# Recurrent heads of a hybrid decoder step: intra-chunk products grouped by tile width, and one weight split moved ahead of the state's scaling

## The chip, the cores and the metric

The kernel runs on one core of a Trainium2 chip. The metric is device time in microseconds (us) of one launch; lower is better. The kernel before takes 1378.13 us, the median of three runs between 1377.38 and 1378.83 us.

## What is computed

The reference is one step of a decoder layer with two parallel branches over 1024 prompt tokens and 8 x 4 sample tokens: a gated linear recurrence (HGRN2, 8 heads with keys and values of 128) and a sliding-window attention. Both branches read one large input projection of the normalised tokens. The change touches the recurrence alone:

```python
def hgrn2_chunk(S, q, k, v, logf):
    b = jnp.cumsum(logf, axis=1)
    diff = b[:, :, None] - b[:, None, :]
    decay = jnp.where(causal, jnp.exp(jnp.where(causal, diff, 0.0)), 0.0)
    att = jnp.einsum('bthk,bshk,btshk->bhts', q, k, decay)
    o = jnp.einsum('bhts,bshv->bthv', att, v) + jnp.einsum('bthk,bhkv->bthv', q * jnp.exp(b), S)
    b_last = b[:, -1]
    k_dec = k * jnp.exp(b_last[:, None] - b)
    S_new = jnp.exp(b_last)[..., None] * S + jnp.einsum('bshk,bshv->bhkv', k_dec, v)
    return S_new, o

h = jnp.einsum('btd,dc->btc', xn, w_in)     # the input projection, 1024 x 8448
```

## The kernel before, in words

Every engine has its own program, written by hand, and the engines meet only through counting semaphores. An order table (class `Steps`, lines 56 to 78) names the steps of each engine, so that `pe.at(now, "os")` is the count that TensorE's semaphore reaches when its step "os" is done. Nothing is scheduled by a tool: each engine works in the order of its code.

**Blocks and slots.** The projections are made in blocks of 128 output columns over all 1056 tokens. A block has three slots of 352 tokens, one PSUM bank each (`pj`), and a slot is 24 matmuls of 128 x 128 by 352 (line 970): 8 slices of the contraction, three passes each, since a 32-bit product is put together from a rounded high part and a rest (`w_h`, `w_l`, `xn_h`, `xn_l`). ScalarE rounds a block's weights into `w_h` (`split_hi`, line 628) and GpSimd subtracts to get `w_l` (`split_lo`, line 556); the first slot of block n waits for both (lines 965 and 966). The buffers are double: `w_h`, `w_l` of block n lie where those of block n-2 lay.

**A recurrent head.** The heads 0 to 7 run one after the other; 1 to 6 are a hardware loop. In each head TensorE (function `head`, lines 1022 to 1111) mixes the small products of the recurrence with the slots of four blocks of projections for the next head: block B(0) (values), B(1) (the forget gate), B(2) and B(3) (query and output gate). The slots fill the time in which VectorE and ScalarE work for the recurrence. The order around the change on TensorE is: slot 1 of B(1); the intra-chunk products (lines 1059 to 1070); slot 2 of B(1); the sample product `ps` and the state updates `u0`, `u1` (line 1079); slots 0 and 1 of B(2); the outputs `o0`, `o1` and the sample outputs `os` (lines 1089 to 1098); slot 2 of B(2); the sample state updates `us0`, `us1` (line 1102); slot 0 of B(3), the first work that needs the weights of B(3); the means of the squares (lines 1108 and 1109, after VectorE's `so1`); slots 1 and 2 of B(3).

**The intra-chunk products.** A chunk is 128 tokens here, and there are 8 of them in two PSUM banks (`ps_a`, `ps_b`). The causal 128 x 128 block of a chunk is built of seven products, each with its own reference point for the decay, so that all exponents stay small: one of 64 x 64 (line 1062, `d64`), two of 32 x 32 next to the diagonal (line 1064, `d32`), four of 32 x 32 on the diagonal (line 1068, `dk`, `dq`). All contract over 128 rows. The output's partitions say which columns of TensorE's array work: the 64 x 64 product uses columns 0 to 63, the two `d32` products use the strips 0 to 31 and 64 to 95, and the four diagonal ones use one strip of 32 columns each. They are plain 32-bit matmuls, and the trace has two weight loads and two matmuls for each product: 16 passes of 64 columns and 96 of 32 columns in a head.

**GpSimd in a head.** The order (function `head`, lines 563 to 583) is: splits of B(0) and B(1); the sample values; `v_exp`; split of B(2); then a wait for TensorE's `os`, the scaling of the sample state (line 579, step "s0e"), and the split of B(3). VectorE adds `us0`, `us1` to the scaled state (line 1515, steps `so0`, `so1`), and between the gates and that it makes the rest of the squares, `sq_l` (line 1509). In the last head ScalarE waits for "s0e" before it rounds the heads' outputs into `hl_h` (lines 751 to 754).

Of the kernel before, what the change touches and what calls it, by code (L numbers as in the profile page):

```python
# [35 lines left out]
P = 128  # L36
# [6 lines left out]
NC = SEQ // P  # L43
# [48 lines left out]
def hybrid_step(nc, x_prompt, x_sample, state_hgrn, cache_k, cache_v, norm_in, w_in, lb_logits, a_gnorm,  # L92
# [84 lines left out]
    with ctx:  # L177
        def sb(name, shape, dt=F32, where=ctx):
            return where.enter_context(nc.sbuf_tensor(name, shape, dt))
# [6 lines left out]
        ps_a, ps_b, ps_c, ps_d, ps_e = [ctx.enter_context(nc.psum_tensor(f"ps_{n}", [P, 512], F32)) for n in "abcde"]  # L186
# [38 lines left out]
        d64 = sb("d64", [P, NC, 2, 64], where=area)  # L225
# [324 lines left out]
        @block.gpsimd  # L550
        def _(g):
            def split_lo(B):

                n, p, _ = B
                g.wait_ge(w_hi_ready, n + 1)
                g.tensor_tensor(w_l[p][:], w_raw[p][:], w_h[p][:].bitcast(F32), ALU.subtract).then_inc(w_lo_ready, 1)  # L556

            pro = Blocks(0, 1, 0)
            g.memset(eps[:], EPS).then_inc(pool_done, pool.tick(("pro", 0), "eps"))
            for n in range(3):  # L560
                split_lo(pro(n))

            def head(i):
                B, now = head_blocks(i), now_of(i)
                split_lo(B(0))
                split_lo(B(1))
                if is_first(i):
                    g.wait_ge(masks_loaded, 48)
                g.wait_ge(act_done, act.at(now, "v3_hi2"))

                g.tensor_tensor(v3[NS:2 * NS, :], v_tok[0:NS, NC, :], v3[0:NS, :].bitcast(F32), ALU.subtract).then_inc(pool_done, pool.tick(now, "v3_lo"))
                g.wait_ge(pool_done, pool.at(now, "v3_lo"))
                g.tensor_tensor(v_exp[:], v3[:].bitcast(F32).rearrange("p (o v) -> p o v", o=1).to_broadcast([3 * NS, NB, P]),
                                batch_m[:].rearrange("p (b o) -> p b o", o=1).to_broadcast([3 * NS, NB, P]),
                                ALU.mult).then_inc(pool_done, pool.tick(now, "vexp"))
                split_lo(B(2))

                g.wait_ge(pe_done, pe.at(now, "os"))
                g.tensor_tensor(s0[:], s0[:], E[:, NC:NC + NB].rearrange("p (b o) -> p b o", o=1).to_broadcast([P, NB, P]),  # L579
                                ALU.mult).then_inc(pool_done, pool.tick(now, "s0e"))  # L580
                split_lo(B(3))
                if is_last(i):
                    split_lo(B(4))

            head(0)
            with nc.gpsimd.Fori(1, HEADS - 1) as i:
                head(i)
            head(HEADS - 1)
            with nc.gpsimd.Fori(1, HEADS) as j:
                B = Blocks(GA, 2, j)  # L590
                split_lo(B(1))
                split_lo(B(2))
            for n in range(4):
                split_lo(Blocks(QZ, 2, 0)(n))
            with nc.gpsimd.Fori(0, HEADS - 1) as m:
                B = Blocks(QZ, 2, m)
                split_lo(B(4))
                split_lo(B(5))
            with nc.gpsimd.Fori(0, 4) as j:
                B = Blocks(GB, 2, j)  # L600
                split_lo(B(2))
                split_lo(B(3))

            def wo_split_lo(n):
                c = WO_ORDER[n]
                g.wait_ge(wo_hi_ready, n + 1)
                g.tensor_tensor(wo_at(c, 1), wo_raw[:], wo_at(c, 0).bitcast(F32), ALU.subtract).then_inc(wo_lo_ready, 1)

            wo_split_lo(0)
            for j in range(3):  # L610
                split_lo(Blocks(PB, 2, j)(2))
                split_lo(Blocks(PB, 2, j)(3))
                wo_split_lo(2 * j + 1)
                wo_split_lo(2 * j + 2)
            wo_split_lo(7)
# [342 lines left out]
        def _(t):  # L958
# [63 lines left out]
            def head(i):  # L1022
                B, now = head_blocks(i), now_of(i)
# [32 lines left out]
                gate_slot(1, "v", (act_done, act), 1)  # L1056

                t.wait_ge(dve_done, dve.at(now, "dkm"))
                for n, bank in enumerate((ps_a, ps_b)):
                    for j in range(4):  # L1060
                        c, o = 4 * n + j, j * P
                        nc.tensor.matmul(bank[0:64, o + 64:o + 128], d64[:, c, 0, :], d64[:, c, 1, :], start=True, stop=True)
                        for m in range(2):
                            nc.tensor.matmul(bank[64 * m:64 * m + 32, o + 64 * m + 32:o + 64 * m + 64],
                                             d32[:, 2 * c + m, 0, :], d32[:, 2 * c + m, 1, :], start=True, stop=True)
                        for m in range(4):
                            e = c * P + 32 * m
                            mm = nc.tensor.matmul(bank[32 * m:32 * m + 32, o + 32 * m:o + 32 * m + 32],
                                                  dk[:, e:e + 32], dq[:, e:e + 32], start=True, stop=True)
                    mm.then_inc(pe_done, pe.tick(now, f"p{n}"))  # L1070
# [5 lines left out]
                for n, bank in enumerate((ps_c, ps_d)):  # L1076
                    for j in range(4):
                        c = 4 * n + j
# [7 lines left out]
                for n, bank in enumerate((ps_e, ps_c)):  # L1086
                    for j in range(4):
                        c = 4 * n + j
# [12 lines left out]
                for n, bank in enumerate((ps_a, ps_b)):  # L1101
                    nc.tensor.matmul(bank[:, :], k3[:, :], v_exp[:, 4 * n:4 * n + 4, :].rearrange("p b v -> p (b v)"),
                                     start=True, stop=True).then_inc(pe_done, pe.tick(now, f"us{n}"))
# [7 lines left out]
                gate_slot(3, "q", (dve_done, dve), 2)  # L1111

            head(0)
            with nc.tensor.Fori(1, HEADS - 1) as i:
                head(i)
            head(HEADS - 1)


            t.wait_ge(act_done, act.at(("last", 0), "sg2"))
            slots(Blocks(GA, 2, 0)(1), hl_h, hl_l, split="last")  # L1120
            with nc.tensor.Fori(1, HEADS) as j:
                B = Blocks(GA, 2, j)
# [15 lines left out]
            for n, bank in enumerate((ps_a, ps_b)):  # L1138
                for j in range(4):
                    c = 4 * n + j  # L1140
# [95 lines left out]
            for u in range(4):  # L1236
                h, grp = u // 2, u % 2
                rows_h = slice(h * HD, (h + 1) * HD)
                bank, o = (ps_c, ps_d)[h], grp * 2 * P
# [18 lines left out]
            for u in range(4):  # L1258
# [3 lines left out]
                for j in range(4):  # L1262
                    o = grp * P + 32 * j
                    mm = nc.tensor.matmul(ps_e[rows_h, o:o + 32], cv[:, 4 * grp + j, rows_h], PT_s[:, u, 32 * j:32 * j + 32],
                                          start=False, stop=True, skip_group_check=True)
# [3 lines left out]
            with nc.tensor.Fori(1, 3) as j:  # L1269
                B = Blocks(GB, 2, j)  # L1270
# [18 lines left out]
            with nc.tensor.Fori(1, 3) as j:  # L1289
                B = Blocks(PB, 2, j)  # L1290
# [444 lines left out]
```

## Time and profile before

| | |
|---|---|
| median of three runs | 1378.13 us |
| span of the profiled execution, first to last instruction | 1374.8 us |
| what lies around the span (median less span) | 3.3 us |
| TensorE busy in the span | 1324.7 us, 96% |
| GpSimd busy | 259.8 us, 19% |
| mean granted TensorE clock | 0.991 of full speed |
| the eight recurrent heads | about 60 us to 565 us of the span |

Times in the rows are us from the span's start unless marked ns. PE is a TensorE matmul, PEld its weight load, DVE VectorE, ACT ScalarE, POOL GpSimd. The records of matmuls overlap, since the array is a pipeline, and their ends are modelled: what a matmul costs is read from the distance between starts. A matmul of 352 columns is recorded with 0.32 us, but one starts every 0.16 us. "x6" in a timeline means that six like instructions are merged into one row, from the first one's start to the last one's end.

### The profile page before, as it was taken

How to read it: one execution, taken by the hardware profiler on the slowest of the kernel's cores; microseconds unless marked ns; L12 is line 12 of the kernel's file. 1: busy time of each engine (PE TensorE's matmuls, PEld its weight loads, DVE VectorE, ACT ScalarE, POOL GpSimd, SP SyncE). 2: the span in 40 equal slices, each digit the busy share in tenths (PEclk: the TensorE clock that was granted, in tenths of full speed). 3: DMA queues.
4: the chain of work that ended last, by engine and by line, in shares of the span. 5: the costliest groups of instructions: out<-in, count | busy, mean ns of one | idle time of the engine just before them, and what ended most of it. 6: DMA issues, size and time to landing. Idle time of an engine off the chain costs nothing.

```text
span 1374.8 us, 23499 instructions
## 1 busy us (share of the span) xinstructions
PE 1324.7 (96%) x9150; PEld 1252.4 (91%) x9150; DVE 602.9 (44%) x1239; ACT 519.1 (38%) x1022; POOL 259.8 (19%) x119
## 2 busy tenths in 40 slices
PE   5799999999999999999999999999999999999998
PEld 4799999999999999899999988988988899999885
DVE  6636566574746465500000444555554400445222
ACT  6343635445353535511111434455444422313111
POOL 0222222222322222222222111011011022242000
PEclk9899999999999999999999999999999999999999
DMA  5212121202021221111112310111110312141231
GB/s 190 64 31 64 32 64 32 76 17 76 17 76 47 62 63 34 49 44 46 46 46 51 81 31 15 31 31 24 22 31 1 87 33 61 46 113 41 92 129 47
DMA packets 136750, 73.61 MB, mean 54 GB/s; under 512 B 37185, under 2 KB 133138, under 8 KB 136690
## 3 DMA queue, kind: packets, MB, share of 16 engines
q1 hardware_dynamic: 136706, 72.99, 19.0%
q8 instruction: 31, 0.51, 0.2%
q14 instruction: 13, 0.11, 0.0%
HBM read 63.77 MB, written 10.22 MB: 54 GB/s over the span
## 4 chain that ended last, share of the span: by engine, by line
PE 67%; issue 22%; POOL 5%; ACT 3%; DVE 3%; DMA 0%; SPq 0%; DVEq 0%; POOLq 0%; ACTq 0%
PE pj L970 46%; POOL w_l L556 4%; PE pj L986 3%; PE pj L1311 2%; PE ps_d L1201 1%; PE ps_e L1201 1%; PE ps_a L1311 1%; PE ps_e L1311 1%; PE ps_b L1189 1%; PE ps_c L1311 1%; PE ps_d L1311 1%; PE ps_b L1311 1%; PE ps_a L1189 1%; PE ps_a L1166 1%; PE ps_c L1189 1%
## 5 line engine op out<-in xcount | busy, mean ns | idle before, releaser
L970 PE MATMUL pj<-xn_h,w_h 128*128 128x352 f32 x1704 | 562.6, 330 | 10.9 <-DVE q L1384 5.3
L970 PE MATMUL pj<-xn_h,w_l 128*128 128x352 f32 x1704 | 552.0, 324 | 0.0
L970 PE MATMUL pj<-xn_l,w_h 128*128 128x352 f32 x1704 | 551.7, 324 | 0.0
L556 POOL TENSOR_TENSOR w_l<-w_raw,w_h 128x1024 fp32r<-128x1024 f32 x82 | 202.2, 2466 | 731.0 <-ACT w_h L628 731.0
L970 PEld LDWEIGHTS pj<-xn_h,w_h 128*128 128x128 f32 x1704 | 324.3, 190 | 15.7 <-DVE q L1384 5.6
L970 PEld LDWEIGHTS pj<-xn_l,w_h 128*128 128x128 f32 x1704 | 324.8, 191 | 0.3
L970 PEld LDWEIGHTS pj<-xn_h,w_l 128*128 128x128 f32 x1704 | 323.7, 190 | 0.0
L628 ACT ACTIVATE w_h<-w_raw 128x1024 fp32r<-128x1024 f32 x82 | 86.4, 1054 | 114.7 <-PE pj L970 99.8
L1546 DVE TENSOR_TENSOR mg<-sg,pj 128x352 f32 (+1 forms) x24 | 12.4, 522 | 151.7 <-PE pj L970 150.2
L837 ACT ACTIVATE scores<-scores,stat 128x256 f32<-128x256 f32 (+1 forms) x128 | 61.4, 481 | 0.0
L970 PE MATMUL pj<-hl_h,w_l 128*128 128x352 f32 x168 | 54.3, 323 | 0.0
L970 PE MATMUL pj<-hl_l,w_h 128*128 128x352 f32 x168 | 54.3, 323 | 0.0
L970 PE MATMUL pj<-hl_h,w_h 128*128 128x352 f32 x168 | 54.0, 322 | 0.0
L1384 DVE TENSOR_TENSOR zs<-zs,pj 128x352 f32<-128x352 f32 x24 | 12.5, 522 | 83.5 <-ACT zs L659 83.5
L1384 DVE TENSOR_TENSOR zb<-zb,pj 128x352 f32<-128x352 f32 x24 | 12.5, 521 | 83.5 <-ACT zb L659 83.5
L579 POOL TENSOR_TENSOR s<-s,E 128x1024 f32<-128x1024 f32 x8 | 15.2, 1897 | 173.0 <-PE ps_d L1097 173.0
L659 ACT ACTIVATE zs<-pj 128x352 f32<-128x352 f32 x24 | 11.1, 464 | 95.3 <-PE pj L970 95.3
L659 ACT ACTIVATE zb<-pj 128x352 f32<-128x352 f32 x24 | 11.1, 464 | 90.0 <-PE pj L970 90.0
L951 ACT ACTIVATE y_sq<-y_o 128x1024 f32<-128x1024 f32 (+1 forms) x9 | 9.5, 1060 | 79.7 <-DVE y_o L1674 79.7
L1389 DVE TENSOR_TENSOR xn_l<-hb,xn_h 128x1056 fp32r<-128x1056 f32 x8 | 10.3, 1304 | 63.3 <-ACT xn_h L667 63.2
L659 ACT ACTIVATE k<-pj 128x352 f32<-128x352 f32 x24 | 11.0, 464 | 70.1 <-PE pj L970 70.1
L659 ACT ACTIVATE sg<-pj 128x352 f32<-128x352 f32 x24 | 10.9, 464 | 66.6 <-PE pj L970 66.6
(363 smaller groups left out, 2095.6 us busy)
## 6 DMA issues: line engine op xcount, KB each, us to landing
w_raw<-in_w_in_dram SPq DMA_DIRECT2D x132, 256.0 KB, 3.4
x_t<-in_x_prompt_dram SPq DMA_DIRECT2D x8, 512.0 KB, 8.5
s<-in_state_hgrn_dram SPq DMA_DIRECT2D x8, 512.0 KB, 4.2
out_dram<-s SPq DMA_DIRECT2D x8, 512.0 KB, 3.2
w_raw<-in_w_pa_dram SPq DMA_DIRECT2D x16, 256.0 KB, 2.9
w_raw<-in_w_pb_dram SPq DMA_DIRECT2D x16, 256.0 KB, 4.4
wo_raw<-in_w_out_dram SPq DMA_DIRECT2D x8, 512.0 KB, 4.0
x_o<-in_x_prompt_dram SPq DMA_DIRECT2D x8, 512.0 KB, 4.1
```

Of the source, the lines that this page charges most:

```text
L556: g.tensor_tensor(w_l[p][:], w_raw[p][:], w_h[p][:].bitcast(F32), ALU.subtract).then_inc(w_lo_ready, 1)
L579: g.tensor_tensor(s0[:], s0[:], E[:, NC:NC + NB].rearrange("p (b o) -> p b o", o=1).to_broadcast([P, NB, P]), ALU.mult).then_inc(pool_done ...
L628: a.activation(w_h[p][:], w_raw[p][:], ACT.Copy).then_inc(w_hi_ready, 1)
L659: a.activation(out[:, span(g)], pj[g][:, 0:W], ACT.Sigmoid).then_inc(act_done, act.tick(where, f"{name}{g}"))
L837: a.activation(scores[:, u, keys], scores[:, u, keys], ACT.Exp, bias=stat[:, 1, u:u + 1], accum_out=stat[:, 3, u:u + 1]).then_inc(act_done ...
L970: mm = nc.tensor.matmul(pj[g][:, 0:W], w[:, kt, :], x[:, kt, span(g)], start=(kt == 0 and m == 0), stop=(kt == KT - 1 and m == 2))
L986: mm = nc.tensor.matmul(pj[g][:, 0:W], w[:, kt, :], x[:, kt, span(g)], start=(kt == 0 and m == 0), stop=(kt == KT - 1 and m == 2))
L1166: mm = nc.tensor.matmul(bank[:, o + lo:o + 2 * P], qT[:, n * P:(n + 1) * P], kT[:, h, (n - 1) * P + lo:(n + 1) * P], start=True, stop=True)
L1189: mm = nc.tensor.transpose(bank[:, o:o + P], scores[:, 2 * n + h, w * P:(w + 1) * P], ident[:, :])
L1201: mm = nc.tensor.matmul(bank[rows_h, o:o + P], v_tk[:, n - 1 + w, rows_h], PT[:, n % 3, 2 * h + w, :], start=(w == 0 or n == 0), stop=(w = ...
L1311: mm = nc.tensor.matmul(bank_of(n, m)[0:r, :], x[:, kt, cols], wo_rhs(m, lo, kt), start=(kt == 0 and i == 0), stop=(kt == KT - 1 and i == 2))
L1384: tt(out[:, span(g)], out[:, span(g)], pj[g][:, 0:W], ALU.mult).then_inc(dve_done, dve.tick(where, f"{name}{g}"))
```

## The change

Two edits, both in the recurrent heads.

On TensorE the eight 64 x 64 products of a head are issued first, for both banks, and then, chunk by chunk, the six products of 32 columns. The products, their operands and their destinations are the same; the semaphore steps `p0` and `p1` still follow the last product of each bank.

On GpSimd the split of B(3) is issued before the wait for `os` and the scaling of the state, not behind them.

```diff
                 split_lo(B(2))
+                split_lo(B(3))
 
                 g.wait_ge(pe_done, pe.at(now, "os"))
                 g.tensor_tensor(s0[:], s0[:], E[:, NC:NC + NB].rearrange("p (b o) -> p b o", o=1).to_broadcast([P, NB, P]),
                                 ALU.mult).then_inc(pool_done, pool.tick(now, "s0e"))
-                split_lo(B(3))
                 if is_last(i):
                     split_lo(B(4))
...
                 t.wait_ge(dve_done, dve.at(now, "dkm"))
+                for c in range(NC):
+                    bank, o = (ps_a, ps_b)[c // 4], c % 4 * P
+                    nc.tensor.matmul(bank[0:64, o + 64:o + 128], d64[:, c, 0, :], d64[:, c, 1, :], start=True, stop=True)
                 for n, bank in enumerate((ps_a, ps_b)):
                     for j in range(4):
                         c, o = 4 * n + j, j * P
-                        nc.tensor.matmul(bank[0:64, o + 64:o + 128], d64[:, c, 0, :], d64[:, c, 1, :], start=True, stop=True)
                         for m in range(2):
                             nc.tensor.matmul(bank[64 * m:64 * m + 32, o + 64 * m + 32:o + 64 * m + 64],
                                              d32[:, 2 * c + m, 0, :], d32[:, 2 * c + m, 1, :], start=True, stop=True)
```

On TensorE, in the first head, the intra-chunk products stand like this before (`x2` is two like products; the six rows show two of the eight chunks):

```order
L970 MATMUL pj<-xn_h,w_l 128x352
L1062 MATMUL ps_a<-d 64x64
L1064 MATMUL ps_a<-d 32x32 x2
L1068 MATMUL ps_a<-dq,dk 32x32 x4
L1062 MATMUL ps_a<-d 64x64
L1064 MATMUL ps_a<-d 32x32 x2
```

And like this after it (line numbers from here on are larger by two, and the 64 x 64 product is line 1061 now):

```order
L970 MATMUL pj<-xn_h,w_l 128x352
L1061 MATMUL ps_a<-d 64x64 x4
L1061 MATMUL ps_b<-d 64x64 x4
L1066 MATMUL ps_a<-d 32x32 x2
L1070 MATMUL ps_a<-dq,dk 32x32 x4
L1066 MATMUL ps_a<-d 32x32 x2
```

The width of the products changed 15 times within a head's group, and now changes once.

On GpSimd, in the loop over the heads 1 to 6, the difference is this (the tensor `s` is the sample state `s0`, and each `w_l` row is the split of one block; the rows `ISA` and `REGISTER_ALU` set up waits and addresses):

```order
 L555 REGISTER_ALU
 L556 TENSOR_TENSOR w_l<-w_raw,w_h 128x1024
-L578 ISA
-L579 TENSOR_TENSOR s<-s,E 128x1024
 L555 REGISTER_ALU
 L556 TENSOR_TENSOR w_l<-w_raw,w_h 128x1024
+L579 ISA
+L580 TENSOR_TENSOR s<-s,E 128x1024
 L586 REGISTER_ALU
```

The scaling now stands last, behind the splits of B(2) and B(3). In the last head the split of B(4) still follows it.

## Rows read from the trace of the kernel before

**Rows 1.** The page, parts 1 and 4: busy time, and the chain that ended last

```profile
PE 1324.7 (96%) x9150; PEld 1252.4 (91%) x9150; DVE 602.9 (44%) x1239; ACT 519.1 (38%) x1022; POOL 259.8 (19%) x119
...
PE 67%; issue 22%; POOL 5%; ACT 3%; DVE 3%; DMA 0%; SPq 0%; DVEq 0%; POOLq 0%; ACTq 0%
```

**Rows 2.** Who TensorE waited for, 60 to 600 us: total, times, longest

```profile
PE pj L970 <- DVE q L1384: 5.3, 1, 5.3
PE ps_a L1108 <- DVE s L1515: 2.3, 1, 2.3
PE pj L970 <- POOL w_l L556: 2.2, 4, 0.5
```

**Rows 3.** Timeline of TensorE in head 2: start us, us, engine, line, what

```profile
221.16 0.32 PE L970 MATMUL pj<-xn_h,w_l 128*128 128x352 f32 x1
221.41 0.33 PE L1062 MATMUL ps_a<-d 128*64 128x64 f32 x2
221.66 0.23 PE L1064 MATMUL ps_a<-d 128*32 128x32 f32 x2
...
221.74 0.24 PE L1068 MATMUL ps_a<-dq,dk 128*32 128x32 f32 x6
221.91 0.33 PE L1062 MATMUL ps_a<-d 128*64 128x64 f32 x2
...
225.46 0.43 PE L970 MATMUL pj<-xn_h,w_h 128*128 128x352 f32 x1
```

**Rows 4.** Lines 1062 and 1068: durations in ns, least, median, most

```profile
L1062 PE MATMUL ps_a<-d x64: 221/246/272, 95.8 to 536.6; 128*64 128x64 f32 x64
L1068 PE MATMUL ps_a<-dq,dk x256: 195/196/218, 96.1 to 536.9; 128*32 128x32 f32 x128
```

**Rows 5.** Timeline near 1100 us, and line 1264: 64-column products back to back

```profile
1100.30 0.65 PE L1264 MATMUL ps_e<-PT,cv 128*64 128x32 f32 x8
...
L1264 PE MATMUL ps_e<-PT,cv x32: 222/223/297, 1100.3 to 1103.6; 128*64 128x32 f32 x32
```

**Rows 6.** Timeline of GpSimd in head 2

```profile
221.02 2.35 POOL L556 TENSOR_TENSOR w_l<-w_raw,w_h 128x1024 fp32r<-128x1024 f32 x1
245.01 1.90 POOL L579 TENSOR_TENSOR s<-s,E 128x1024 f32<-128x1024 f32 x1 [21.64 <-PE ps_d L1097]
246.87 2.84 POOL L556 TENSOR_TENSOR w_l<-w_raw,w_h 128x1024 fp32r<-128x1024 f32 x1
```

**Rows 7.** Timeline of TensorE in head 2, before the first slot of B(3)

```profile
248.69 0.40 PE L1102 MATMUL ps_a<-v_exp,k 96*128 96x512 f32 x1
248.93 0.39 PE L1102 MATMUL ps_b<-v_exp,k 96*128 96x512 f32 x1
249.85 0.40 PE L970 MATMUL pj<-xn_h,w_h 128*128 128x352 f32 x1 [0.54 <-POOL w_l L556]
```

**Rows 8.** Timeline of ScalarE in head 2: the rounding of the weights of B(3)

```profile
233.97 1.06 ACT L628 ACTIVATE w_h<-w_raw 128x1024 fp32r<-128x1024 f32 x1
```

**Rows 9.** Timeline of VectorE in head 2

```profile
220.19 3.26 DVE L1470 CAST k<-k_tok 32x128 fp32r<-32x128 f32 x1
223.48 0.22 DVE L1471 CAST k<-k_tok 32x128 fp32r<-32x128 f32 x1
...
235.29 0.81 DVE L1401 TENSOR_SCALAR k<-k,noml,oml 128x1056 f32<-128x1056 f32 x1
...
244.36 0.51 DVE L1384 TENSOR_TENSOR q<-q,pj 128x352 f32<-128x352 f32 x1
...
246.27 4.09 DVE L1509 TENSOR_TENSOR sq_l<-vT,sq_h 128x512 fp32r<-128x512 f32 x3
...
251.31 0.67 DVE L1515 TENSOR_TENSOR s<-s,ps_b 128x512 f32<-128x512 f32 x1
```

**Rows 10.** Stretches behind `os`, heads 0, 2, 3, 6; third from the end: granted clock

```profile
120.40:123.80 3.40, 3.40 (x13) 3.40 (x13) 3.40 (x4) 0.00 (x0) 3.40 (x2) 0.50 0.00 0
244.80:248.60 3.80, 3.80 (x26) 3.80 (x26) 3.80 (x6) 0.64 (x3) 3.59 (x2) 1.00 0.00 0
308.10:311.50 3.40, 3.40 (x14) 3.40 (x12) 3.40 (x4) 0.00 (x0) 3.40 (x2) 0.50 0.00 0
495.90:499.20 3.30, 3.30 (x13) 3.30 (x12) 3.30 (x5) 0.16 (x1) 3.30 (x2) 0.50 0.00 0
```

**Rows 11.** The chain that ended last, in order of time, last head

```profile
558.60 1.91 POOL s L579
560.51 0.02 issue
560.53 3.04 ACT hl_h L667 x3
```

## The prediction

> **What bounds the kernel.** I read the page's busy times and its last chain first. TensorE is busy for 1324.7 of 1374.8 us and holds most of the chain; no other engine is over 44% [rows 1]. So a microsecond that leaves TensorE's program leaves the time, unless another engine's result then comes late. Next the view of who waited for whom: over all eight heads TensorE stood still for 5.3 us once, at the heads' start, for 2.3 us once in the last head, and four times for some 0.5 us for GpSimd's `w_l` [rows 2]. Then the timelines of one loop head, head 2, engine by engine, for the two places of the change. TensorE is a pipeline, so I take distances between starts, not durations.
>
> **Intra-chunk products before.** The group begins at 221.41 and the next slot at 225.46 us: 4.05 us for eight chunks, 0.506 each, which is also the distance between the first two 64-column rows up to their rounding (221.41, 221.91) [rows 3]. Inside a chunk: the pair of 64-column passes is merged into 0.33 us, and its last pass lasts 0.22 [rows 3, 4], so the second starts 0.11 after the first, at 221.52. The first 32-column pass starts at 221.66, 0.14 to 0.15 later. The row of six 32-column passes ends at 221.98 and one lasts 0.196, so the last pass starts near 221.79: twelve passes start within 0.13 us. The next 64-column pass starts 0.12 later. So a chunk is 0.11 (64) + 0.15 (to 32) + 0.13 (32) + 0.12 (back to 64). The two changes of width are over half of it, although no semaphore stands there.
>
> **Intra-chunk products after.** Four terms for a head.
> - Sixteen 64-column passes in a row. The trace before has no such row, but near 1100 us eight passes with weights of the same width follow each other in the same 64 columns, over all 128 rows: 0.65 us less a duration of 0.22, by seven, is 0.061 us each [rows 5]. These stream only 32 columns where ours stream 64. The upper bound is the distance in today's pair, 0.11, in which nothing ran ahead. I take 0.11 for the first step and 0.06 for the other fourteen, 0.95 us, since the row near 1100 is the one in a steady run; bounds 0.90 and 15 x 0.107 = 1.60.
> - One change to 32 columns: 0.15.
> - Ninety-six 32-column passes. In a chunk the strips 0 and 2 take four passes each and the others two, so the strips 0 and 2 decide: four passes start within 0.13 us, three steps of 0.043 on average, the first of which has to wait for its first weights. Half of 0.06, as the weights are half as wide, would be 0.03 each in a steady run, 0.12 a chunk. I take 0.125 for seven chunks and 0.13 for the last, 1.0 us; bounds 0.94 and 7 x 0.17 + 0.13 = 1.32.
> - The change to the slot's width, as today: 0.12.
>
> Together 2.22 us (2.11 to 3.19) against 4.05. A head gives 1.83 us (0.86 to 1.94), and eight give 14.6 (6.9 to 15.5).
>
> One rule speaks against the first term. The row says 0.061 us from pass to pass with every pass over the same 128 rows [rows 5]. The Trainium skill (TensorE: Matmul & The Clock Gate, Part 3, the mechanism of packing) has a weight load overlap with running matmuls only if their row groups differ. By that rule the sixteen passes would stay at 0.107, and the sum would be 8 x 0.65 = 5.2 us smaller; by the row it is as above, and the row disagrees with the rule. A second one: the twelve 32-column passes start within 0.13 us, 11 ns each [rows 3, 4]. The same page (Part 1, on the matmul gap) lets no matmul start within 25 ns of the last, which would make 96 passes 2.4 us and the whole gain of this edit 8 x 0.43 = 3.4 us; the rows contradict that already for one chunk.
>
> **Is anything late when TensorE is 1.8 us earlier?** What follows the group in TensorE's order waits for results that were ready long before. The next slot of B(1) has its weights already. VectorE's `k_tok` copies end before 220.2, and its sample keys soon after 223.7 [rows 9], against a need after 229. The split of B(2) runs from 221.02 to 223.37 [rows 6] and is first read one slot and the state updates later, 6 us behind the group's end. From there on VectorE starts its state chain on TensorE's `u0`, and ScalarE its sigmoids on the slots, so they move up together with TensorE. I cost this at nothing; the cover is these several microseconds.
>
> **The split of B(3).** In head 2 TensorE issues the second `us` product at 248.93 and the next slot only at 249.85; a 512-column product takes 0.24 to the next start (248.69 to 248.93), so 0.69 us are lost [rows 7] (the waits view says 0.54, as it counts from modelled ends). The split ends at 246.87 + 2.84 = 249.71 [rows 6], which is what ended the wait. After the change it can start when ScalarE's rounding is done, 233.97 + 1.06 = 235.03 [rows 8], and is over near 237.4, 12 us ahead of its use. What is late next is VectorE's first query gate, ready at 244.87 [rows 9], against 249.16: 4.3 us to spare. So the whole 0.69 goes, in the four heads that have it [rows 2]: 2.8 us. In heads 0, 3 and 6 TensorE runs at half clock behind `os` [rows 10] and comes late itself; there the split was hidden. The last head gains nothing here: its chain goes from `os` over the scaling to ScalarE's `hl_h` [rows 11], and the 2.3 us wait for `so1` is shorter than what ScalarE needs in any case.
>
> The scaling gets a new neighbour in front. It waits for `os`, which is done at 245.0, and the split is over 7.6 us sooner, so it is not delayed.
>
> **What the split collides with.** GpSimd slows VectorE. A copy of 32 x 128 took 3.26 us beside `v_exp` and the split of B(2), and its twin right behind 0.22 [rows 9, 6]; `sq_l` took 4.09 beside the scaling and the split of B(3). The split's new place lies on VectorE's `kf` (235.29, 0.81 us), which it may hold up for at most its own length, 2.4 us; the query gate then comes at 247.1 at the latest, still 2 us early. In return `sq_l` is free once the scaling ends at 246.9, about 2 us sooner. `so1` is ready at 251.98 today and stays near 252.1 if both happen; TensorE asks for it one slot, 24 x 0.16 = 3.9 us, behind 249.16, at 253.05 (26 matmuls in 3.80 us, the edges included [rows 10]). One microsecond of room: thin, but nothing is lost. Bounds for this whole edit: 0 (the gain eaten by VectorE) and 4.1 us (all six loop heads had it to give, if no clock drop hid it).
>
> **The clock.** The granted clock was 0.5 for 3.4 us behind `os` in three of the eight heads, and 1.00 in the same place of head 2 [rows 10]. That is the level of 1.2 GHz instead of 2.4. Right before these stretches TensorE ran `o`, the small sample products of `os` and little else. A drop costs half of 3.4 us less its edges, about 1.6. Which heads it hits will be another draw when a head is 2.5 us shorter. I leave the count at three and carry one more or one less, 1.6 us either way, in the range; in a head that newly drops, nothing else is lost.
>
> **Sum.** 14.6 + 2.8 = 17.4 us off the profiled execution's span of 1374.8: 1357.4. The 3.3 us around the span stay, as their sum with it is the median of the runs: 1360.7 us.
>
> **Rivals.**
> - *No running ahead in the 64-column passes.* They stay 0.107 apart, as in today's pair, because the next weights are not loaded beside a pass of 64 streamed columns. Against it: the run near 1100 us. For it: those passes stream half as much. 5.2 us more: 1365.9. 15%.
> - *The split's gain is lost.* VectorE held up in its new place brings `so1` or the query gate to TensorE later than the 1 us of room. For it: the 3.26 us copy. 2.8 us more: 1363.5. 10%.
> - *The order of widths is not what costs.* The 0.15 and 0.12 us would belong to each chunk, for its first weights, and come back at each chunk of the grouped passes. Only the split's 2.8 us stay: 1375.3. Against it: inside the 32-column part the new weights of `dq`, `dk` follow `d` without any such gap. 4%.
> - *Slower.* The clock drops in every head, and twice: behind the grouped narrow passes and behind `os`. From 3 drops to 16 is 13 x 1.6 = 20.8 us, against 17.4 gained: 1381.5. It decides from 11 additional drops on. Against it: the group today, narrow passes for 4 us, has the full clock in every head's trace, and the new one is denser. 3%.
>
> **Numbers.** The forecast has 68%, with its own range 1358.4 to 1362.6 (one clock drop more or less, and the bounds of the 32-column term). The range for 8 in 10 reaches up over the first rival's time, with one drop less than it would need in full, and down by one drop and the better bounds: 1358.0 to 1366.5. About 0.2%, 2.8 us, is what a measurement here can tell from none. Faster 95%, within 0.2% 2% (part of the third rival), slower 3%.
>
> **What the profile after would show.** The group from its first 64-column pass to the next slot takes 2.2 us, with the 64-column passes 0.06 apart; 2.9 us would be the first rival, 4.0 the third. TensorE has no wait for `w_l` in the heads, and the distance from the second `us` product to the next slot is 0.24. GpSimd's split of B(3) lies some 9 us ahead of the scaling, and `sq_l` falls to about 2 us. `kf` grows, to 3 us at most. A new wait of TensorE on VectorE's `so1`, in loop heads, or more than five stretches of half clock would make the prediction wrong.

## The result: 9 us faster, where 17.4 were forecast

| | median | lowest to highest | runs | profiled span |
|---|---|---|---|---|
| before, same chip | 1377.89 us | 1375.81 to 1380.78 | 6 | 1374.8 us |
| after | 1368.81 us | 1366.78 to 1373.44 | 6 | 1366.8 us |

The ratio is 0.9938 [0.9924, 0.9952]. The change makes the kernel faster, and the time lies above the forecast's range (1358.0 to 1366.5 us). The mean granted clock of TensorE is 0.985, where it was 0.991 before.

**Busy time.** Part 1 of the page of the kernel after, against [rows 1]:

```profile
PE 1314.7 (96%) x9150; PEld 1249.0 (91%) x9150; DVE 611.9 (45%) x1239; ACT 519.4 (38%) x1022; POOL 260.0 (19%) x119
```

TensorE is busy for 10.0 us less. VectorE, with the same 1239 instructions, is busy for 9.0 us more: a first sign that it is held up.

**The group of intra-chunk products.** TensorE's timeline in head 0 after (start us, us, engine, line, what), against [rows 3]:

```profile
96.03 0.32 PE L970 MATMUL pj<-xn_h,w_l 128*128 128x352 f32 x1
96.29 0.68 PE L1061 MATMUL ps_a<-d 128*64 128x64 f32 x8
96.80 0.63 PE L1061 MATMUL ps_b<-d 128*64 128x64 f32 x8
97.36 0.22 PE L1066 MATMUL ps_a<-d 128*32 128x32 f32 x2
...
98.50 0.43 PE L970 MATMUL pj<-xn_h,w_h 128*128 128x352 f32 x1
```

The group now runs from 96.29 to 98.50, 2.21 us where it took 4.05. It is the same in all eight heads. The starts of the single records put the 64-column passes 0.107 us apart once and 0.058 from then on.

**The two places of waiting.** Who TensorE waited for from 60 to 600 us, after (engine, line, for whom: total us, times, longest), against [rows 2]:

```profile
PE pj L970 <- DVE q L1386: 5.5, 1, 5.5
PE ps_a L1110 <- DVE s L1517: 5.4, 3, 2.1
```

`w_l` no longer stands there. But the wait for `so1`, which was one of 2.3 us in the last head, is now three: in the heads 0 and 1, and still in the last. TensorE's timeline behind the `us` products of head 0 after, against [rows 7], shows both:

```profile
121.70 0.40 PE L1104 MATMUL ps_a<-v_exp,k 96*128 96x512 f32 x1
121.94 0.40 PE L1104 MATMUL ps_b<-v_exp,k 96*128 96x512 f32 x1
122.17 0.33 PE L970 MATMUL pj<-xn_h,w_h 128*128 128x352 f32 x1
...
125.83 0.32 PE L970 MATMUL pj<-xn_h,w_l 128*128 128x352 f32 x1
128.22 0.49 PE L1110 MATMUL ps_a<-sq_h,mean_m 128*128 128x512 f32 x1 [2.06 <-DVE s L1517]
```

The slot follows the second `us` product after 0.23 us (0.92 before). The norm's first product follows the slot after 2.39 us, where 0.16 is the step, so 2.23 us are lost. It is the same in head 1.

**The clock.** Stretches behind `os` in heads 0, 1, 2, 3 and 7 after (stretch, its length, busy time and count of TensorE's matmuls, its loads, VectorE, ScalarE, GpSimd; then the granted clock), against [rows 10]:

```profile
118.00:121.70 3.70, 3.70 (x24) 3.70 (x24) 3.67 (x5) 0.62 (x3) 2.31 (x1) 1.00 0.00 0
184.00:187.40 3.40, 3.40 (x22) 3.32 (x21) 3.40 (x5) 1.41 (x2) 1.92 (x1) 1.00 0.00 0
243.40:246.80 3.40, 3.40 (x14) 3.40 (x13) 3.37 (x5) 0.00 (x0) 1.18 (x1) 0.51 0.00 0
304.90:308.30 3.40, 3.40 (x14) 3.40 (x12) 3.37 (x5) 0.00 (x0) 1.12 (x1) 0.50 0.00 0
...
550.60:554.00 3.40, 3.40 (x14) 3.40 (x13) 1.97 (x3) 2.65 (x3) 0.72 (x1) 0.51 0.00 0
```

At 1.00 TensorE ran at 2.4 GHz, at 0.50 at 1.2. Before, three heads had the low level there; now six have it, the heads 2 to 7, and each begins 61.4 us after the last. Such a stretch of half clock is called a drop from here on.

**Where the time went.** The distances between the first `us` products of successive heads, read from TensorE's timelines, sum this up. A head in which nothing is lost takes 61.70 us before (62.39 less the 0.69 for `w_l`) and 1.84 less after, 59.86. Most heads after last 61.43 and have a drop, so a drop costs 1.57. The wait for `so1` costs 2.23, and 59.86 + 2.23 is the first distance after, 62.09.

| us from head to head | 0-1 | 1-2 | 2-3 | 3-4 | 4-5 | 5-6 | 6-7 | sum |
|---|---|---|---|---|---|---|---|---|
| before | 61.65 | 62.39 | 63.95 | 61.73 | 62.38 | 63.98 | 61.55 | 437.6 |
| after | 62.09 | 63.73 | 61.43 | 61.48 | 61.53 | 61.32 | 61.39 | 433.0 |

After minus before over these seven: 7 x -1.84 = -12.9 for the group, 4 x -0.69 = -2.8 for `w_l`, 2 x 2.23 = +4.5 for `so1`, and 6 drops in place of 2 in this stretch, +6.3. The sum is -4.9, and -4.6 was measured. Ahead of it, to the first `us` product, 2.9 us are gone (head 0's group gives 1.84 of them and its drop 1.57; 0.5 us more are spent elsewhere), and behind the last 0.4. Together that is the 8.0 us between the spans.

### The profile page after: what moved, and what is told of

It is laid out like the page before. It is cut to its first block, busy times and chain, and to the rows that moved or that the text cites. A ratio compares the mean times of both kernels' runs of the same rounds, so it can differ in the third digit from the quotient of the medians.

```text
span 1366.8 us, 23499 instructions
## 1 busy us (share of the span) xinstructions
PE 1314.7 (96%) x9150; PEld 1249.0 (91%) x9150; DVE 611.9 (45%) x1239; ACT 519.4 (38%) x1022; POOL 260.0 (19%) x119
## 4 chain that ended last, share of the span: by engine, by line
PE 56%; issue 1%; DVE 1%; ACT 1%; DVEq 0%; ACTq 0%
PE pj L970 37%; PE pj L986 3%; PE pj L1313 2%; PE ps_d L1203 1%; PE ps_e L1203 1%; PE ps_a L1313 1%; PE ps_e L1313 1%; PE ps_b L1191 1%; PE ps_c L1313 1%; PE ps_d L1313 1%; PE ps_b L1313 1%; PE ps_a L1191 1%; PE ps_a L1168 1%; PE ps_c L1191 1%; PE ps_b L1168 1%
## 5 line engine op out<-in xcount | busy, mean ns | idle before, releaser
L556 POOL TENSOR_TENSOR w_l<-w_raw,w_h 128x1024 fp32r<-128x1024 f32 x82 | 199.2, 2429 | 832.3 <-ACT w_h L628 832.3
L837 ACT ACTIVATE scores<-scores,stat 128x256 f32<-128x256 f32 (+1 forms) x128 | 61.4, 481 | 0.0
L1581 DVE TENSOR_SCALAR scores<-scores,stat 128x256 f32<-128x256 f32 (+1 forms) x128 | 35.5, 341 | 1.1
L1654 DVE TENSOR_TENSOR sgb<-sgb,pj 128x352 f32 (+1 forms) x24 | 12.5, 520 | 47.2 <-PE pj L970 38.3
```

The source lines that it names most:

```text
L837: a.activation(scores[:, u, keys], scores[:, u, keys], ACT.Exp, bias=stat[:, 1, u:u + 1], accum_out=stat[:, 3, u:u + 1]).then_inc(act_done ...
L1581: v.tensor_scalar(target[:, u, keys(u)], target[:, u, keys(u)], st[:, 4, u:u + 1], None, ALU.mult).then_inc(dve_done, dve.tick(now, f"n{u}"))
```

## What held VectorE up

`kf` is the operation at L1403, which scales and shifts the next head's `k`; VectorE starts its work on the next head's exponents with it. In head 0 after, GpSimd's timeline (in brackets the idle time before) and then VectorE's, against [rows 6, 9]:

```profile
108.12 2.39 POOL L556 TENSOR_TENSOR w_l<-w_raw,w_h 128x1024 fp32r<-128x1024 f32 x1 [9.83 <-ACT w_h L628]
118.03 2.31 POOL L580 TENSOR_TENSOR s<-s,E 128x1024 f32<-128x1024 f32 x1 [7.51 <-PE ps_d L1099]
123.40 2.50 POOL L556 TENSOR_TENSOR w_l<-w_raw,w_h 128x1024 fp32r<-128x1024 f32 x1 [3.06 <-ACT w_h L628]
```

```profile
108.19 2.89 DVE L1403 TENSOR_SCALAR k<-k,noml,oml 128x1056 f32<-128x1056 f32 x1
...
118.49 1.89 DVE L1428 SCALAR_TENSOR_TENSOR dk<-cs,b 128x32 f32<-128x32 f32 x1
...
122.95 3.59 DVE L1511 TENSOR_TENSOR sq_l<-vT,sq_h 128x512 fp32r<-128x512 f32 x3
...
127.50 0.68 DVE L1517 TENSOR_TENSOR s<-s,ps_b 128x512 f32<-128x512 f32 x1
```

`kf` starts 0.07 us behind the split of B(3) and ends 0.58 us after it: 2.89 us for work of 0.81. From there VectorE is 2.1 us late, and so a small operation on 128 x 32 (L1428), 0.18 us in head 2 before, where nothing is beside it, meets the scaling and takes 1.89. Then `sq_l` starts so late that GpSimd has begun the next head's first split, and takes 3.59. Measured from the first `us` product, `kf` starts as before (13.5 us ahead of it), and `so1` is ready 6.48 us behind it, where it was 3.29. The difference, 3.2 us, is +2.08 for `kf`, +1.71 for the small operation and -0.50 for `sq_l`.

The Trainium skill (SBUF — State Buffer, "SBUF: two separate sides") says that VectorE and GpSimd have one pair of ports in common, an exclusive lock: of a GpSimd operation and a VectorE operation with two inputs in SBUF (if the GpSimd one reads SBUF) or in a two-port mode, the one that starts first holds the pair to its end, and the other waits. These rows agree for `kf` and the small operation in the main: each started behind GpSimd's and ended with it or behind it, the first 0.58 us behind the split's end (110.51), the second 0.04 behind the scaling's (120.34). By the page an operation would still have its own work to do once the lock is free, which as an estimate makes `kf` end 0.81 us behind the split, at 111.32, and not at 111.08; the rows are that much shorter. Operations with one of two inputs in PSUM are not on the page's list; the third experiment below has a row for that.

## Experiments

The runs of before beside them had medians of 1380.3 to 1380.6 us.

**Each edit alone.** The first kernel has TensorE's edit only.

> Only the 64-column products are moved together; GpSimd's order is that of the kernel before. Theory A (the split in its new place delays VectorE, and that makes TensorE wait for so1): no wait for so1 in the loop heads, kf back at 0.8 us, the wait for w_l of 0.7 us back in heads without a clock drop; 8 x 1.84 = 14.7 us less than before, less up to 0.9 for each further clock drop, so about 1360 to 1364 us by the three-run median of before. Theory B (it is the earlier TensorE that outruns VectorE): so1 is waited for as in the changed kernel, 2.2 us in each head without a drop, and the time is 1367 to 1370 us.

The second has GpSimd's only.

> Only GpSimd's split of B(3) is moved; TensorE's products stand as before. Theory A: 0.7 us of w_l wait goes and 2.2 us of waiting for so1 comes in every head without a clock drop, so slower than before: with five such heads some 8 us, 1383 to 1387 us, and less the more heads have a drop. Theory B: no wait for so1, since TensorE comes as late as before, and 2 to 3 us less than before, about 1375 us.

| | median | lowest to highest | against before |
|---|---|---|---|
| group only | 1364.14 us | 1363.51 to 1367.55 | 0.9893 [0.9878, 0.9908] |
| split only | 1387.49 us | 1383.14 to 1388.82 | 1.0047 [1.0032, 1.0062] |

So the second edit makes the kernel slower by itself, and the change is slower with it than without. Who TensorE waited for, 60 to 600 us, in the first and in the second:

```profile
PE pj L970 <- DVE q L1386: 5.3, 1, 5.3
PE ps_a L1110 <- DVE s L1517: 1.2, 1, 1.2
PE pj L970 <- POOL w_l L556: 0.5, 1, 0.5
```

```profile
PE ps_a L1108 <- DVE s L1515: 7.5, 4, 2.1
PE pj L970 <- DVE q L1384: 5.4, 1, 5.4
```

Without the moved split no loop head waits for `so1` (the one wait is the last head's); but of its eight heads only head 0 has no drop, and only there could the wait have shown: `so1` is ready 3.3 us behind the first `us` product, as before. The second kernel says more. Its TensorE stands as before, where heads 1, 2, 4 and 5 had neither a drop nor this wait. With the split moved alone three loop heads wait, 1, 3 and 5, all those without a drop behind `os`, and VectorE's rows of head 1 there are the same pair:

```profile
174.12 2.79 DVE L1401 TENSOR_SCALAR k<-k,noml,oml 128x1056 f32<-128x1056 f32 x1
...
184.33 1.89 DVE L1426 SCALAR_TENSOR_TENSOR dk<-cs,b 128x32 f32<-128x32 f32 x1
```

That settles the wait: it comes from the split's new place, not from a faster TensorE. It does not settle the clock: the kernel with the group alone has seven drops, from 178.2 on and each 61.4 us after the last, and still is 16.2 us faster than before by the medians. Its profile also lost 2.6 us less than before behind the last head, where the one drop that most of these kernels have near 1100 us is absent; from 1000 to 1200 us, in the changed kernel and in this one:

```profile
1000.00:1200.00 200.00, 192.87 (x1316) 183.85 (x1315) 68.47 (x198) 71.14 (x161) 35.85 (x15) 0.98 0.17 45
```

```profile
1000.00:1200.00 200.00, 192.86 (x1334) 183.88 (x1332) 70.09 (x199) 72.76 (x162) 38.51 (x17) 1.00 0.19 50
```

The kernel with the split alone has five drops in the heads. Four lie behind `os`, in the heads 0, 2, 4 and 6; the fifth begins at 322.8 us, 1.5 us after head 3's wait of 2.1 us for `so1` was over. Heads 1 and 5 have the same wait and no such drop.

**The split under the state chain.** With both edits in, ScalarE here rounds B(3) before it takes the logarithm for the next head, so that GpSimd's split falls on VectorE's state chain, which reads PSUM.

```diff
-                log_f(now, i + 1)
                 split_hi(B(3))
+                log_f(now, i + 1)
```

> The changed kernel, and ScalarE rounds the weights of B(3) ahead of the logarithm of the forget gate, so that the split of B(3) starts some 3.5 us sooner, while VectorE works on the state chain out of PSUM. Theory A says that VectorE is held up only where it reads SBUF alone: kf falls from 2.8 to 0.8 us, the small operation at dk beside the scaling from 1.9 to 0.2, so1 is not waited for in the loop heads, and undropped heads last 59.9 us. With six clock drops about 1365 us, with three 1361. If GpSimd's work delays VectorE wherever it lies, the state chain grows by 2.4 us and so1 stays late: 1368 us or more.

1365.75 us (1362.50 to 1368.62, 5 runs), 0.9895 [0.9878, 0.9912]. No loop head waits for `w_l` or `so1`. GpSimd's split of B(3) in head 2 and VectorE's rows there:

```profile
224.94 2.40 POOL L556 TENSOR_TENSOR w_l<-w_raw,w_h 128x1024 fp32r<-128x1024 f32 x1 [5.85 <-ACT w_h L628]
...
225.05 1.12 DVE L1489 SCALAR_TENSOR_TENSOR S<-S,E,ps_c 128x128 f32<-128x128 f32 x3
...
229.14 0.80 DVE L1403 TENSOR_SCALAR k<-k,noml,oml 128x1056 f32<-128x1056 f32 x1
...
237.37 0.18 DVE L1428 SCALAR_TENSOR_TENSOR dk<-cs,b 128x32 f32<-128x32 f32 x1
...
240.12 1.89 DVE L1511 TENSOR_TENSOR sq_l<-vT,sq_h 128x512 fp32r<-128x512 f32 x3
```

The same three steps in head 0 of the changed kernel, with nothing beside them:

```profile
104.22 1.11 DVE L1489 SCALAR_TENSOR_TENSOR S<-S,E,ps_c 128x128 f32<-128x128 f32 x3
```

The state chain's three steps take 1.12 us beside the split and 1.11 without it; they read one operand from PSUM and are not held up. `kf` and the small operation are back at their own lengths. This removes 2 x 2.23 us of waits, yet against the changed kernel the heads' stretch is only 3.2 us shorter (429.8 against 433.0), because the drops go from six to seven: every head from head 1 on has one.

**Why does every head have a drop?** The distance of 61.4 us is the length of a head with a drop, 59.86 + 1.57. So one theory was that the drop of a head brings the next head to the same place in the same time, and so on. A rival was that the small products in themselves bring it in every head. For this the third kernel got padding: the first matmul of one slot is repeated five times in each head.

```diff
-            def slot(B, g, xh=xn_h, xl=xn_l):
+            def slot(B, g, xh=xn_h, xl=xn_l, again=0):
...
+                for _ in range(again):
+                    nc.tensor.matmul(pj[g][:, 0:W], w_h[p][:, 0, :], xh[:, 0, span(g)], start=True, stop=True)
...
-                    slot(B(0), g)
+                    slot(B(0), g, again=5 if g == 2 else 0)
```

> As the kernel that rounds first, and in each head the first matmul of the last value slot is done six times instead of once: five more matmuls of 0.16 us, 0.8 us a head, with the same output. Theory L (a head with a clock drop lasts 61.4 us, and by chance that brings the next head to the same place, so that the drop comes again in each): a head with a drop now lasts 62.2 us, the chain of drops breaks, three or so heads have one, and the time is only 1 to 3 us above the kernel that rounds first, though 6.4 us of matmuls were added. Theory D (the denser intra-chunk group, or the earlier split, brings the drops in every head): seven drops again, and 6.4 us more.

1365.88 us (1364.16 to 1367.10, 4 runs), 0.9899 [0.9884, 0.9915]. 6.4 us of matmuls were added, and by the medians the time is that of the kernel without them. By the profiles the heads are 1.6 us longer (1.0 to the first `us` product and 0.6 from there to the last), which the stretch near 1100 us hides: the profile without padding has a drop there and this one none. The stretches behind `os` in the heads 1 to 6, except 5:

```profile
178.60:182.00 3.40, 3.40 (x25) 3.40 (x25) 3.40 (x7) 0.65 (x3) 1.90 (x1) 1.00 0.00 0
240.30:243.70 3.40, 3.40 (x13) 3.40 (x13) 3.22 (x7) 0.24 (x1) 1.54 (x1) 0.51 0.00 0
301.50:304.90 3.40, 3.40 (x24) 3.40 (x24) 3.40 (x6) 0.64 (x3) 1.90 (x1) 1.00 0.00 0
363.20:366.60 3.40, 3.40 (x13) 3.40 (x13) 3.05 (x6) 0.07 (x1) 1.37 (x1) 0.50 0.00 0
...
486.10:489.50 3.40, 3.40 (x14) 3.40 (x13) 2.97 (x6) 0.00 (x0) 1.29 (x1) 0.50 0.00 0
```

The drops come in the heads 2, 4 and 6, and in the last; seven have become four, and the distances are 60.6 and 62.1 us in turn (59.86 and the 0.8 of the padding, with a drop or without). The mean granted clock is 0.989 to 0.990 in all four runs, where the kernel without padding had 0.983 to 0.987, which fits fewer drops in the other runs too. The rival is out: the same small products stand in every head, and three loop heads in six have no drop. That a head's length decides is borne out, but not the theory as it stands. Heads 6 and 7 both have a drop, 61.4 us apart, though head 6 to 7 lasts 62.1. And in the kernel with two groups of products, further down, a head with a drop lasts 61.6 us, yet its drops still begin 61.4 us apart, each 0.2 us earlier in its head than the last, until head 5 has none. So 61.4 us is not just what a head happens to last. What it is in the chip that ties the drops to this distance stays open.

**Wide matmuls between the small products.** The nine small sample products of `os` are what TensorE does ahead of a drop: in the kernels that have them in a row, the drops behind `os` begin 0.1 to 1.6 us after the last of them. In this kernel, built on the third, one 352-column matmul of the next slot stands before each of the eight that read `s0`; in a second one, two.

```diff
+                turns = []
+                gate_slot(2, "sf", (act_done, act), 2, turns)
                 nc.tensor.matmul(ps_d[:, 0:NS], v_tok[0:NS, NC, :], att_s[:, :], start=True, stop=True)
                 for m in range(NB):
                     e = SEQ + DEC * m
+                    turns.pop(0)()
                     mm = nc.tensor.matmul(ps_d[:, DEC * m:DEC * (m + 1)], s0[:, m, :], qI[:, e:e + DEC], start=False, stop=True, skip_group_check=True)
                 mm.then_inc(pe_done, pe.tick(now, "os"))
-                gate_slot(2, "sf", (act_done, act), 2)
+                for turn_ in turns:
+                    turn_()
```

> As the one that rounds first, and the eight small products of the sample state (4 columns each) alternate with the first eight matmuls of the following slot of B(2). If the small products in a row are what the clock drop needs, no drop comes in the heads, each of which then lasts 59.9 us: 1357 us or a little under. If drops come from something else in the head, their number stays at three to six and the time at that of the kernel that rounds first, plus up to 0.1 us a head for changing operands.

With one: 1363.33 us (1360.53 to 1363.89, 4 runs), 0.9869 [0.9854, 0.9885]. Drops in the first two loop heads only and one of 6.8 us in the last; the five head-to-head distances without one are 59.74 to 59.93. Its ratio is not clear of the third kernel's (0.9895 [0.9878, 0.9912]).

> As the interleaved kernel, with two slot matmuls behind each of the first eight small products, so that TensorE streams 352 columns for 0.32 of each 0.54 us there. If the small products in a row are what a drop needs, no head but perhaps the last has one, loop heads last 59.8 us, and the time is 2 to 4 us under the kernel with one matmul between. If drops come from another place, two to six remain at the time of that kernel.

With two: 1373.48 us (1371.55 to 1375.22, 6 runs), 0.9952 [0.9939, 0.9965]. Not one drop in the loop heads, as expected, and that at a head's length of 61.5 to 61.7 us, near the one at which the kernels without interleaving had a drop in nearly every head. But the time missed what was expected by far. Who TensorE waited for there, 60 to 600 us:

```profile
PE ps_a L1124 <- DVE s L1531: 12.8, 8, 2.6
PE pj L971 <- DVE q L1400: 5.5, 1, 5.5
PE pj L995 <- ACT sg L659: 1.8, 1, 1.8
```

`os` comes later, so VectorE idles before the sample gate and reaches `sq_l` when GpSimd scales (243.91 to 245.81); its last part, of 32 columns, then meets the next head's first split (246.74 to 249.23) and takes 2.40 us. VectorE's rows, head 2:

```profile
244.29 0.25 DVE L1515 SCALAR_TENSOR_TENSOR ha<-ps_d,par,zs 128x32 f32 x1 [1.77 <-ACT sq_h L739]
244.46 4.82 DVE L1525 TENSOR_TENSOR sq_l<-vT,sq_h 128x512 fp32r<-128x512 f32 x3
```

The loop heads are 1.7 us above 59.86 each: a price as high as that of a drop, in every head.

**Both, put right.** The last design keeps two matmuls per small product and lets VectorE make the two large parts of `sq_l` before the sample gate, while GpSimd is still idle.

```diff
-    gated_head = ["gate0", "gate1", "gates", "sl0", "sl1", "sls"]
+    gated_head = ["gate0", "gate1", "sl0", "sl1", "gates", "sls"]
...
-                gate("gates", "shs", ps_d, slice(SEQ, T), slice(0, NS))
...
+                    if n == "s":
+                        gate("gates", "shs", ps_d, slice(SEQ, T), slice(0, NS))
```

> As the kernel with two slot matmuls between the small products, and VectorE makes the rests of the first two thirds of the squares before it waits for the sample part of the gate, in the 1.8 us in which it stood idle there and before the scaling of the state starts on GpSimd. If so1 was late because the rests fell beside GpSimd's scaling and split, the wait of 1.6 us in each head goes, loop heads last 59.8 us without a clock drop, and the time falls by 8 x 1.6 = 13 us from that kernel, to 1360 us or a little under: the fastest. If so1 is late because the sample products end later, the wait stays above 1 us.

1361.15 us (1359.70 to 1361.76, 4 runs), 0.9859 [0.9843, 0.9875], the lowest median and ratio of all, though the interval overlaps that of the kernel with one matmul between (0.9869 [0.9854, 0.9885]). VectorE's rows in head 2, where the scaling began at 241.39:

```profile
239.89 1.29 DVE L1526 TENSOR_TENSOR sq_l<-vT,sq_h 128x512 fp32r<-128x512 f32 x2
241.77 0.25 DVE L1515 SCALAR_TENSOR_TENSOR ha<-ps_d,par,zs 128x32 f32 x1 [0.59 <-ACT sq_h L739]
241.94 1.40 DVE L1526 TENSOR_TENSOR sq_l<-vT,sq_h 128x32 fp32r<-128x32 f32 x1
```

All seven head-to-head distances are 59.76 to 59.86 us. Their sum is 418.7, 18.9 us below before: 12.9 for the groups, 2.8 for `w_l` and 2 x 1.57 for the drops. So the forecast's gains were all there to be had in the loop. Behind the last head's `us` product 5.6 us are given back: by longer waits (1.5 us for `so1` and 2.9 for ScalarE, where before lost 2.3 and 0.3 there), by a stretch of 6.8 us at half clock that before did not have, and by one near 1100 us that is 6.8 us long where it was 3.4. The first of these stretches:

```profile
545.80:552.60 6.80, 4.71 (x16) 4.71 (x17) 3.83 (x4) 6.73 (x11) 0.00 (x0) 0.50 0.39 106
```

**What a change of width costs.** The third kernel with the 64-column passes grouped by bank, so three changes of width in place of one.

```diff
-                for c in range(NC):
-                    bank, o = (ps_a, ps_b)[c // 4], c % 4 * P
-                    nc.tensor.matmul(bank[0:64, o + 64:o + 128], d64[:, c, 0, :], d64[:, c, 1, :], start=True, stop=True)
                 for n, bank in enumerate((ps_a, ps_b)):
+                    for c in range(4 * n, 4 * n + 4):
+                        o = c % 4 * P
+                        nc.tensor.matmul(bank[0:64, o + 64:o + 128], d64[:, c, 0, :], d64[:, c, 1, :], start=True, stop=True)
```

> As the kernel that rounds first, with the 64-column products grouped bank by bank: four of 64 columns, the 24 of 32 columns of that bank, and again for the second bank. Three changes of width instead of one. If a change of width and back costs what it did between chunks (0.15 + 0.13 us, less the 0.06 and 0.03 of a normal step, and the first pair's slower start), the group takes 2.21 + 0.25 = 2.46 us a head. If the first weights of each chunk were the cost, it would take 2.21.

TensorE in head 0:

```profile
96.04 0.68 PE L1062 MATMUL ps_a<-d 128*64 128x64 f32 x8
...
97.28 0.68 PE L1062 MATMUL ps_b<-d 128*64 128x64 f32 x8
...
98.52 0.43 PE L970 MATMUL pj<-xn_h,w_h 128*128 128x352 f32 x1
```

2.48 us against 2.21: two more changes cost 0.27. The 64-column products, the same eight, are not what cost before, the changes are. A change of width is a change of the array's columns here too (0 to 63 against single strips of 32); no run parts the two. (The kernel's one time was 1366.05 us.)

**The changed kernel again**, unchanged, beside the last design.

> The changed kernel again, unchanged, on the chip of this call. The waits for so1 in heads without a clock drop and the drops share the heads between them as before: 0.991 to 0.995 of the kernel before.

1370.33 us (1365.75 to 1374.93, 6 runs), 0.9926 [0.9906, 0.9946]. Waits for `so1` in the heads 0 and 1 and drops in 2 to 7, as in the first profile.

## Why the prediction was wrong, point by point

The prediction named two signs of being wrong, a new wait for `so1` in loop heads and more than five stretches of half clock, and both came.

- **The group: right.** 2.22 us forecast, 2.21 measured. The step of the 64-column passes was taken as 0.11 once and 0.06 from then on, and is 0.107 and 0.058. The rule of the Trainium skill that was weighed against it (TensorE: Matmul & The Clock Gate, Part 3, the mechanism) does not hold here, nor does the least distance of 25 ns of its Part 1: the twelve 32-column passes of a chunk take 0.127 us, 11 ns each. The change to 32 columns is 0.15 and that back 0.13. The eight heads give 14.7 us (14.6 forecast).
- **The wait for `w_l`: right.** 0.69 us in each of four heads are gone, and the slot follows after 0.23. But a drop hides this wait as well: the kernel with the group alone, with seven drops, had it in head 0 only. Once the heads have drops, the moved split has little to give.
- **The split's collision: the step that failed.** The prediction said that `kf` may be held up by 2.4 us and that "`sq_l` is free once the scaling ends at 246.9", with "One microsecond of room" left. The first half was right (2.08). (Its 247.1 us for the query gate does not follow from 244.87 and 2.4, which give 247.3; nothing hangs on it.) But it followed only `kf` and the query gate, and did not move the operations between them: 2 us later they lie under the scaling, where an operation of 0.18 us takes 1.89, and `sq_l` then meets the next head's split. `so1` came 3.2 us later against the `us` products where the prediction had it 0.1 later: past the room by 2.2, +4.5 us in two heads. This is the rival "The split's gain is lost", which had 10% and was priced too low: it charged only the 2.8 us of lost gain, and nothing for a wait longer than the one it replaces. The experiments with one edit each show it: no such wait in a loop head without the moved split, three with it alone, and 7.1 us more by the medians.
- **In the other heads this was hidden by a drop**, which slows TensorE and not VectorE: `sq_l` is then over before GpSimd's next split, and `so1` is ready 2.7 us behind the `us` product. A head with a drop is 1.57 us longer and one with the wait 2.23. So a run with more drops need not be slower: of the six runs after the two with the highest clock (0.992, 0.989) are the two slowest (1373.44 and 1372.54 us), and when the changed kernel ran again, the slowest (1374.93 us) had the highest clock (0.991).
- **The clock: missed.** "I leave the count at three and carry one more or one less". There were six, +4.7 us, with a price per drop as forecast (1.57 against 1.6). What was wrong was to treat them as draws of their own: a drop in one head goes with one in the next, here. The count alone would have given 1360.7 + 4.7 = 1365.4 us, inside the range; with `so1` it is past it. The two terms are not independent either: with fewer drops more heads would have shown the wait, at 2.23 us each, so the miss does not hang on this draw of the clock.

Sum for the profile: -17.5 for what was right, +4.5 for `so1`, +4.7 for three drops more, +0.3 for the rest, which is what the others leave: -8.0.

## What to carry to other kernels

- When VectorE is made late by a collision with GpSimd, shift everything that follows on VectorE by it and look for the next collision: the hold-up grows (2.1 us became 3.8) before any engine waits. Better is a place where VectorE reads PSUM or GpSimd has nothing to do.
- Group TensorE's products by width; a change of width costs 0.13 to 0.15 us here, as much as the six products of 32 columns of a chunk.
- Put wide matmuls between tiny ones, if no other engine waits for what the tiny ones make (with two between them each head lost 1.6 us to such a wait, until VectorE's order was changed). And after any change of a loop's length look at the granted clock in every pass of the loop: a gain of 1.8 us in a head can be answered by a drop of 1.6 in each.

## What was unexpected of the hardware

- 6.4 us of added matmuls cost nothing in the median (1365.88 against 1365.75 us) and 1.6 us in the heads of the profile, since they broke the row of drops.
- One operation on 32 columns, work of 0.18 us, took 1.89 us beside GpSimd and ended 0.04 us behind GpSimd's operation. Another of the same width, the last part of `sq_l` in the kernel with two matmuls between, took 2.40. The price went by what was left of GpSimd's operation, not by their own size.
- TensorE fell to half clock within 1.6 us of nine tiny products, though the trace shows no idle time there. With two wide matmuls between them it did not do so in any of the heads 0 to 6, in two kernels.
